# One transformer layer: order of loads, weight splits and factor sums in the opening of the projection

## What is computed

```
m = silu(c) @ w_ada + b_ada; shift, scale, gate = split(m, 3)   # for both kinds of tokens
h = rms(x, norm_w) * (1 + scale) + shift
z = h @ w_in                    # 4096 columns: q, k, v, two gates, three conv inputs
q, k = rms(q), rms(k), rotary on the latent tokens; k and v also joined with cached ones
att = softmax(q0 k0) v - lam * softmax(q1 k1) v, per head
y = x + gate * (concat(rms(att) * silu(g_att), cb * conv(cc * ch) * silu(g_conv)) @ w_out)
```

## Time and profile before

| | |
|---|---|
| median of 3 runs | 1892.68 us (1891.6 to 1893.28) |
| profiled execution | 1895.1 us, its span in the trace 1893.3 us |
| mean granted TensorE clock | 0.97 of full speed |
| TensorE (matmuls) busy | 1703.5 us, 90% |
| VectorE / ScalarE / GpSimd busy | 1166.0 / 721.4 / 749.7 us |
| DMA | 163.69 MB, mean 86 GB/s |
| one load of rows or transposed tokens | 1024 KB |
| one weight block, one gate block | 512 KB |

### The profile page before, as it was taken

One profiled execution on the slowest core, in us unless ns is written; L12 is line 12 of the kernel. 1 busy time (PEld: TensorE's weight loads), 2 busy tenths in 40 slices (PEclk: granted clock), 3 DMA queues, 4 the chain that ended last, 5 costly groups with the idle time before them and its releaser, 6 DMA issues.

```text
span 1893.3 us, 25309 instructions
## 1 busy us (share of the span) xinstructions
PE 1703.5 (90%) x8526; PEld 1461.0 (77%) x8526; DVE 1166.0 (62%) x1521; ACT 721.4 (38%) x1531; POOL 749.7 (40%) x615
## 2 busy tenths in 40 slices
PE   3899999989999999996688888888888888669999
PEld 1688888879989999895477777777777777558889
DVE  2553888832422323324888888888888888556553
ACT  4562333320000101001666666666666666321110
POOL 0002888830000000000877777777777777400000
PEclk8899999999999999998999999999999999879999
DMA  9862322230120201105400321031001110156441
GB/s 352 271 195 85 108 102 96 99 113 30 36 72 20 92 19 42 48 29 133 106 29 28 68 60 31 28 75 51 28 29 50 55 30 11 58 187 239 161 144 48
DMA packets 131473, 163.69 MB, mean 86 GB/s; under 512 B 10464, under 2 KB 119776, under 8 KB 130272
## 3 DMA queue, kind: packets, MB, share of 16 engines
q1 hardware_dynamic: 126288, 158.61, 25.9%
q10 hardware_dynamic: 5136, 4.46, 0.7%
HBM read 112.95 MB, written 50.07 MB: 86 GB/s over the span
## 4 chain that ended last, share of the span: by engine, by line
PE 69%; DVE 17%; issue 5%; DMA 4%; SPq 3%; ACT 1%; POOL 1%; DVEq 0%; ACTq 0%; POOLq 0%
PE ps L685 37%; PE ps L910 10%; PE ps L835 8%; DVE e L1463 8%; PE ps L824 8%; PE ps L816 4%; DVE stt L1481 2%; DVE at L1456 1%; PE ps L749 1%; DMA scr<-in_xT 1%; PE ps L893 1%; DMA worw<-in_w_out 1%; DMA spill_cv<-scr 1%; DMA qb<-spill_q 1%; DVE stt L1512 1%
## 5 line engine op out<-in xcount | busy, mean ns | idle before, releaser
L685 PE MATMUL ps<-hT,w 128*128 128x448 f32 (+1 forms) x3360 | 689.6, 365 | 11.5 <-DVE w L1247 11.5
L685 PEld LDWEIGHTS ps<-hT,w 128*128 128x128 f32 x3360 | 623.0, 188 | 71.5 <-issue 26.0
L1146 ACT ACTIVATE e<-ps,stt 128x1024 f32<-128x1024 f32 x256 | 285.8, 1116 | 258.0 <-DVE stt L1481 257.7
L835 PE MATMUL ps<-kb,qb 128*128 (+1 forms) x1280 | 336.9, 394 | 49.5 <-ACT e L1146 30.9
L1481 DVE TENSOR_REDUCE stt<-ps 128x1 f32<-128x1024 f32 x256 | 312.3, 1221 | 95.0 <-PE ps L835 94.6
L824 PE MATMUL ps<-at,vb 128*128 128x256 f32 x1088 | 279.4, 388 | 9.2 <-ACT atto L1107 9.2
L835 PEld LDWEIGHTS ps<-kb,qb 128*128 128x128 f32 x1280 | 206.5, 193 | 86.0 <-ACT e L1146 39.5
L643 POOL TENSOR_TENSOR stt<-stt,lamc 128x2 f32<-128x2 f32 x64 | 12.6, 197 | 653.9 <-DVE stt L1499 653.9
L650 POOL TENSOR_TENSOR e<-e,stt 128x1024 f32<-128x1024 f32 (+1 forms) x192 | 262.9, 1398 | 5.0
L824 PEld LDWEIGHTS ps<-at,vb 128*128 128x128 f32 x1088 | 209.4, 196 | 47.9 <-issue 9.7
L816 PE MATMUL ps<-cst,e 128*128 128x128 f32 x1088 | 175.1, 279 | 59.9 <-DVE at L1456 59.3
(11 more groups left out here) (120 smaller groups left out, 1297.3 us busy)
## 6 DMA issues: line engine op xcount, KB each, us to landing
raw<-in_w_in SPq DMA_DIRECT2D x32, 512.0 KB, 3.7
qb<-spill_q SPq DMA_DIRECT2D x256, 64.0 KB, 2.3
scr<-in_xtok SPq DMA_DIRECT2D x8, 1024.0 KB, 8.0
wad<-in_w_ada SPq DMA_DIRECT2D x4, 2048.0 KB, 17.0
scr<-in_xT SPq DMA_DIRECT2D x8, 1024.0 KB, 6.2
kb<-spill_k SPq DMA_DIRECT2D x8, 1024.0 KB, 9.7
spill_k<-scr SPq DMA_DIRECT2D x32, 224.0 KB, 2.2
spill_q<-scr SPq DMA_DIRECT2D x32, 224.0 KB, 2.2
```

Of the source, the lines that this page charges most:

```text
L685: mm = pe.matmul(out, slot_of(l, j), rhs_of(r, j), start=(i == 0 and j == 0), stop=(i == 2 and j == DJ - 1))
L835: mm = pe.matmul(out[:, c0 - k0:c1 - k0], qb[:, t, ver, m], keys, start=(ver == 0), stop=(ver == 1))
L1146: act.activation(dst[:, c * 1024:(c + 1) * 1024], ps[:, 2 * c:2 * c + 2, :].rearrange("p c n -> p (c n)"), ACT.Exp, bias=stt[:, b, 0, 3 * ...
```

## The change

Four edits. SP issues the transposed tokens of group 0 ahead of weight blocks 2 and 3, where they came behind. SP waits for the squares of group 1 and issues the rows of group 2 ahead of the six gate blocks, where they came behind. TensorE spreads the factors of group 1 between the second and the third pass of tile 0, where it did so behind tile 0. And ScalarE and VectorE round and split weight block 3 later: ScalarE rounds it behind the scaling of group 0, VectorE takes its residue between the rounding and the residue of group 0's tokens. Nothing is added to what is computed. Line numbers behind the edits grow by 2 to 4 (L685 becomes L687, L989 becomes L990, L1294 becomes L1295, L1296 becomes L1300, L714 becomes L716).

```diff
--- before.py
+++ after.py
@@ -363,9 +363,9 @@
                 load_ada(hf)
             load_w(0, 0)
             load_w(1, 1)
+            load_xs(0)
             for i in range(2):
                 sp.dma_start(raw2[:, i], a["w_in"][2 + i]).then_inc(s_raw2[i], 16)
-            load_xs(0)
             sp.wait_ge(sq_ready, 1)
             load_xt(1)
             load_xs(1)
@@ -377,10 +377,10 @@
             sp.wait_ge(mod_cp, 4)
             sp.wait_ge(mod_tr, 4)
             sp.wait_ge(w_lo, 4)
+            sp.wait_ge(sq_ready, 2)
+            load_xt(2)
             load_gate(0)
             load_gate(1)
-            sp.wait_ge(sq_ready, 2)
-            load_xt(2)
 
             for c in range(4, 6):
                 sp.wait_ge(w_lo, c - 3)
@@ -681,6 +681,8 @@
                         pe.wait_ge(parts[i // 2], ready)
                     if parts and ready == 1 and i < 2:
                         pe.wait_ge((w_hi, w_lo)[i], 4)
+                    if parts and ready == 1 and i == 2:
+                        spread(1)
                     for j in range(DJ):
                         mm = pe.matmul(out, slot_of(l, j), rhs_of(r, j),
                                        start=(i == 0 and j == 0), stop=(i == 2 and j == DJ - 1))
@@ -731,9 +733,7 @@
                     wait(pe, z_used, t - 4)
                     passes(ps[:, t % BANKS, :], lambda l, j: hT[:, l, j, t * P:(t + 1) * P],
                            lambda r, j: w[:, 0:4, r, j, :], (hhi_ready, hlo_ready) if t == 2 * g else None, g + 1)
-                    if t == 0:
-                        spread(1)
-                    elif t == 1 or g > 0 and t == 2 * g and g + 2 < XN:
+                    if t == 1 or g > 0 and t == 2 * g and g + 2 < XN:
                         spread(g + 2)
                     if 1 <= g <= 3:
                         if t == 2 * g:
@@ -972,12 +972,13 @@
             act.activation(r32(vhi), craw[:], ACT.Copy).then_inc(hi_ready, 1)
             for hf in range(4):
                 mod_copy(hf)
-            for c in range(4):
-                if c < 2:
-                    w_split(c, c, c, 1)
-                else:
-                    act.wait_ge(s_raw2[c - 2], 16)
-                    act.activation(w[:, c, 0], raw2[:, c - 2], ACT.Copy).then_inc(w_hi, 1)
+            def w_first(c):
+                act.wait_ge(s_raw2[c - 2], 16)
+                act.activation(w[:, c, 0], raw2[:, c - 2], ACT.Copy).then_inc(w_hi, 1)
+
+            w_split(0, 0, 0, 1)
+            w_split(1, 1, 1, 1)
+            w_first(2)
             for g in range(XN):
                 c0, n = XGROUPS[g]
                 v = 0 if c0 < SAMPLE else 1
@@ -992,6 +993,7 @@
                 for t in tiles[:-1]:
                     v_hi(t)
                 if g == 0:
+                    w_first(3)
                     x_square(1)
                     x_root(1)
                 if g + 2 < XN:
@@ -1285,13 +1287,15 @@
             dve.tensor_tensor(mult[:], mult[:], norm_w.rearrange("p (n o) -> p n o", o=1).to_broadcast([P, DJ, 2]),
                               ALU.mult).then_inc(mod_ch, 1)
             normalize(0)
-            for c in range(2, 4):
-                w_split(c, c % 2, c, raw2)
+            w_split(2, 0, 2, raw2)
             for g in range(XN):
                 c0, n = XGROUPS[g]
                 x = xbuf(g)
                 dve.wait_ge(h32_ready, g + 1)
                 dve.tensor_copy(hT[:, 0, :, c0:c0 + n], x).then_inc(hhi_ready, 1)
+                if g == 0:
+                    w_split(3, 1, 3, raw2)
+                    dve.wait_ge(w_lo, 4)
                 dve.wait_ge(hhi_ready, g + 1)
                 dve.tensor_tensor(hT[:, 1, :, c0:c0 + n], x, f32(hT[:, 0, :, c0:c0 + n]), ALU.subtract)\
                     .then_inc(hlo_ready, 1)
```

## The result

The changed kernel is slower. Its median is 1902.67 us (19 runs, 1898.31 to 1908.8) against 1897.18 us for the kernel before on the same chips (19 runs, 1891.6 to 1902.44). The ratio is 1.0037, 95% interval 1.0024 to 1.0051: some 7 us (the two means differ by 7.1 us, the two medians by 5.5). The forecast was 1894.7 us, no change that can be measured, range 1889.4 to 1897.4. The profiled execution took 1904.49 us, its span is 1902.7 us, TensorE is busy for 1715.8 us.

The account below looks back on a forecast made before the run. TensorE's opening and a load stream were taken to meet without slack at the transposes. Minus 10.7, minus 1.9, 0, plus 2.0 at successive points left 2.0 us on the median 1892.68: 1894.7 us, range 1889.4 to 1897.4.

Parts of the forecast that it names:

- Tile 0, tile 2, factors of group 3: TensorE's opening: tile 0 starts near 43.3 us, tile 2 near 58.3, group 3's factors come near 72.7.
- The gain of some 10 us at the end of tile 2: Tile 2 on TensorE ends near 64.0 us against 74.77: 10.7 won, 8.8 by earlier start, 1.9 by a shorter tile.
- plus 2.0 at the transposes: Last term of the sum: TensorE waits 2.0 us at the gate part's transposes, and this stays until the end.
- The other chain reaches them 14.9 us after 69.4.: Chain from group 3's rows landing at 69.4 us, through group 4's rows, reaches the gate part's transposes at 84.3.
- The clock behind the wait: At the transposes: the 2 us wait might drop TensorE's clock, costing another 1.9 us; left out of the sum.
- the slower rival: The case of a result slower by over 0.2%, from a later stream or a clock drop at the transposes; chance 0.13.
- The gain of part 1: Group 0's transposed tokens ahead of two weight blocks: tile 0 starts 2.8 us earlier, capped at 3.1, possibly nothing.
- Cost nothing; the cover is those two passes: Block 3's later rounding and residue hide behind tile 0's first two passes, with 2 us to spare.
- The queue has room: Rival, chance 0.10: group 3's rows land soon after issue, at 63.9 us; time 3.5 us shorter, 1889.2.
- The stream starts later still: Rival, chance 0.13: tokens gain under 1 us, SP issues 3.8 us later; with nothing gained 4.8 us lost, 1897.5.
- its second branch, the clock: Same slower end if the 2 us wait at the transposes drops TensorE's clock, another 1.9 us; within chance 0.13.
- It doesn't do what it says: Rival, part of 0.77: group 2's rows land late, tile 2 starts as before, 1 to 3 us lost.

Follow-up runs that it names:

- gcopy_all: Changed kernel with all three ScalarE copies of gate parts moved ahead of the squares that stood before them; 1.0019 to the kernel before.
- defer_all: Changed kernel with early gate copies and loads in order of need, three gate blocks and weight blocks 4 and 5 put later; 0.9968 to the kernel before.
- wait_only: Kernel before plus SP waiting for the squares of group 1 before the six gate blocks, no load moved; 1.0020.
- after_again: The changed kernel run and profiled again, nothing altered; 1902.66 us.
- before_again: The kernel before run and profiled again, nothing altered; 1895.73 us.
- moves1: Kernel before with only weight block 3's rounding and residue moved later, no load moved; 1.0034.
- undo3: Changed kernel with the six gate blocks again issued ahead of the rows of group 2, other edits kept; 1.0032 to the kernel before.
- loads1: Kernel before with only the transposed tokens of group 0 issued ahead of weight blocks 2 and 3; 0.9995.
- only2: Kernel before with only the factors of group 1 put inside tile 0; 1.0008.
- only3: Kernel before with only the wait for group 1's squares and the rows of group 2 put ahead of the gate blocks; 1.0027.
- split: Changed kernel with three gate blocks issued ahead of the wait for group 1's squares, the other three behind the rows of group 2; 1.0035 to the kernel before.
- after_nomove: Changed kernel with weight block 3 rounded and split where the kernel before does it; 1.0037 to the kernel before.
- gcopy: Changed kernel with only the first ScalarE gate copy moved ahead of the squares of group 4; 1.0038 to the kernel before.

## Why the prediction was wrong

**Tile 0, tile 2, factors of group 3: right.** Forecast 43.3, 58.3 and 72.7; the two profiles without the late multipliers show 43.40, 57.91 and 72.40, and 43.41, 57.93 and 72.39. The issue was forecast at 45.0 and came at 45.21, the landing of group 3's rows at 69.4 and came at 69.1. The gain of some 10 us at the end of tile 2 is real and lost again by the end of tile 3 (81.7 and 81.8, forecast 82.3), by the mechanism that the prediction names.

**The step that failed is the last term, "plus 2.0 at the transposes", in its size.** The transposes came 2.7, 3.2 and 5.3 us later than 82.31, not 2.0, and the slow tile behind them, which the sum had at nothing, cost another 1.4 to 2.5 us. The mechanism is shown: gcopy_all takes the wait away, defer_all turns the sign, and wait_only shows that a late stream costs with no load moved, there by way of tile 2. Three things were mis-sized:

- *"The other chain reaches them 14.9 us after 69.4."* It took 15.9 us in after_again (69.11 to 85.03), 16.4 and 16.5 in the other two. One link alone took 1.2 us or more longer: group 4's rows land 8.9 to 9.3 us after their issue, not 7.8. In before_again this link took 9.2 us as well, so a row of one profile was taken for fixed.
- *The clock behind the wait.* I gave it to the slower rival and held the clock's 1.00 from 60 to 64 us against it. All three profiles have it: tile 4 takes 8.21, 7.29 and 7.15 us, 1.4 to 2.5 us over 5.73. A window in which the clock had not yet fallen was the wrong row to lean on; the pause at the transposes is followed by a clock of 0.50 while tile 4 runs. The kernel before can do the same: in before_again a wait of 1.74 us there is followed by a tile of 7.06 us.
- *The gain of part 1, "I take 2.8 us".* With the tokens early, late multipliers hold the normalization back, and in the first profile they are 2.6 us late. There SP issues at 47.25, not 45.0. The kernel before hides this behind the tokens' landing; the changed one passes it on to the stream.

Together, the factors ahead of tile 8 come 4.4 to 8.5 us after 115.2, mean 5.0 us between the three profiles of each kernel (121.1 against 116.1), where the forecast had 2.0.

Part of the distance between forecast and result lies outside this sum: the forecast stood on a median of 1892.68 us from 3 runs, and that of 19 runs of the same kernel is 1897.18, itself almost at the upper end of the range. The 2.0 us put on it would have given 1899.2, against 1902.67 measured.

**"Cost nothing; the cover is those two passes"**, said of the moved residue of block 3, was wrong as a statement on its own. Its cover is one pass and not two, since the second pass of tile 0 multiplies with this residue. That cover held: the residue ended at 46.53, and tile 0, begun at 45.45, shows no wait for it. I asked whether TensorE waits for it and not who else does. SP does, and moves1 shows 1.0034 for it alone. In the sum it hid behind the wait for the squares, which ended 0.6 us later (47.15 against 46.53 in the first profile of the changed kernel).

**The rivals.** "The queue has room" is out: wherever the stream kept its loads, rows of group 3 landed 23.8 to 24.6 us behind its start, as in the kernel before (24.4, 23.9 and 24.3). "The stream starts later still" came true by its second branch, the clock. In the first profile its end came too, an issue after 47 us, by another cause: late multipliers, not late tokens. "It doesn't do what it says" is out.

**What stays open.** Behind the factors ahead of tile 8 the rest of the span varies from execution to execution, 1774.6 to 1784.4 us over all 18 profiles, with no difference in the program; most of it lies in the attention (782.0 to 794.1 us from its first score product to the first output product). For the kernel before it is 1776.1 to 1778.0, for the changed one 1779.0 to 1781.3 us. Whether the some 2 us between the stretch's 5.0 and the measured 7 come from there, or are chance of three profiles, the runs don't tell; gcopy_all, as short as before in the stretch and 1.0019 in time, points to the former. For undo3 and moves1 the distance is larger: by their ratios they cost some 6 us, while their factors ahead of tile 8 come 2.2 and 2.8 us after 115.2. Each was profiled in its fastest execution, and what a slower one looks like is not known.

## What to carry to other kernels

Where one queue carried a full stream, reordering its head moved no end here: the last load of the stream landed when it did, plus what the new head waited for. So follow the end of the stream to the engine that needs it. When an instruction is moved, look for every engine that waits on its semaphore, SP's list included. And put what is needed late (here three gate blocks and two weight blocks) behind what is needed soon: together with the gate copies moved out of the way this was worth 6 us, the new head alone was a loss.

## What the runs showed of the hardware

- A load landed later where others were issued closer behind it. Group 4's rows took 7.7 to 8.0 us from issue to landing in seven profiles in which the last two gate blocks were issued 5.1 to 6.0 us behind them (two of the kernel before, loads1, moves1, only2, undo3, wait_only); they took 9.2 us in before_again, with 4.8 us between, and 8.9 to 9.3 us in eight profiles with 2.7 to 3.3 us between (three of the changed kernel, only3, split, after_nomove, gcopy, gcopy_all). SP issues these blocks when TensorE has done the first gate part: at 76.70 in the kernel before (row below, and the earlier trace rows), at 75.89 in before_again, whose tile 2 was 0.4 us shorter. So a TensorE that is ahead of the stream may itself delay the rows that it needs next. That the closeness is the cause is not shown, since no run moves these two blocks alone.

```profile
76.70 1.26 SPq L347 DMA_DIRECT2D wga<-in_w_ada  x2
```

- Six gate blocks in pieces of 512 bytes kept the stream at 296 GB/s in the kernel before and at 304 and 290 GB/s from 52 to 56 and from 56 to 60 us in the changed one, where 408 flowed behind them in the kernel before. The line rate that the Trainium skill ("DMA: Bandwidth & Descriptors", "Specifications") gives for such sizes was seen in neither.
- At the transposes of a gate part, waits of 1.7 to 3.7 us of TensorE were followed each time (eight profiles) by a tile of 7.1 to 8.2 us instead of 5.7 (granted clock 0.50 from 88 to 92 us in the changed kernel's first profile); waits of under 1 us there and elsewhere (defer_all has several) were not. A wait of 1.87 us ahead of tile 2 in only3 was followed by a tile of 5.73 us, so the length of the wait alone doesn't decide.
